# Sixty-four-row transposes for the inverse softmax sums, and a second output bank in the second layer's attention

## The reference

```python
def softmax_f32(s, dtype):
    return jax.nn.softmax(s.astype(jnp.float32), axis=-1).astype(dtype)

# layer of the first block, need_ctx = (it is not the last layer)
ya, yca = global_gqa(px[0], px[1], px[2], pc[0], pc[1], pc[2], cos, sin, qn, kn, need_ctx)
yb, ycb = neighbourhood_attn(px[3], px[4], px[5], pc[3], pc[4], pc[5], rpb, need_ctx)
yc_, ycc = window_gqa(px[6], px[7], px[8], pc[6], pc[7], pc[8], cos, sin, sink, need_ctx)
ux = jnp.concatenate([ya, yb, yc_], axis=-1) * jax.nn.silu(px[9])
x = x + gate[:, None, :] * (ux @ w_out)
```

## Time and profile before

| | us |
|---|---|
| median of 3 runs | 1854.64 |
| lowest, highest | 1851.79, 1855.0 |
| the profiled execution | 1852.03 |
| its span in the trace | 1850.2 |
| PE busy, share of the span | 1817.2, 98% |
| DVE busy, share | 1261.6, 68% |
| ACT busy, share | 1083.4, 59% |
| mean granted clock of PE | 0.997 of full speed |

### The profile page before, as it was taken

How to read it: one execution, slowest core, us unless ns; L and a number is a source line. 1 busy time by engine, 2 the same in 40 slices (tenths; PEclk the granted TensorE clock), 3 DMA queues, 4 the chain that set the end, 5 groups by cost and what they waited for, 6 DMA issues and landing times.

```text
span 1850.2 us, 34397 instructions
## 1 busy us (share of the span) xinstructions
PE 1817.2 (98%) x13400; PEld 1577.4 (85%) x13400; DVE 1261.6 (68%) x2157; ACT 1083.4 (59%) x1907; POOL 55.0 (3%) x57
## 2 busy tenths in 40 slices
PE   7999999999999999999999999999999999999998
PEld 5878878879888978889889988889888889998887
DVE  6663354478726678776686787757776677688765
ACT  5372264385736487764656577746774556567762
POOL 0000000003000000001000000000000000000001
PEclk9999999999999999999999999999999999999999
DMA  9232243242234315555432445554554642355553
GB/s 356 101 115 84 98 157 112 92 145 98 86 113 143 118 67 182 192 194 208 182 115 92 173 179 194 181 199 173 191 187 173 220 156 93 137 182 182 182 184 134
DMA packets 42571, 285.49 MB, mean 154 GB/s; under 512 B 4944, under 2 KB 6352, under 8 KB 9424
## 3 DMA queue, kind: packets, MB, share of 16 engines
q1 hardware_dynamic: 40832, 278.24, 41.9%
q0 software_dynamic: 1616, 5.52, 0.9%
HBM read 282.69 MB, written 1.05 MB: 153 GB/s over the span
## 4 chain that ended last, share of the span: by engine, by line
PE 92%; ACT 3%; DVE 2%; issue 1%; DMA 1%; SPq 0%; POOL 0%; DVEq 0%; ACTq 0%
PE bank L2340 25%; PE bank L2334 14%; PE bank L2335 13%; PE bank L2336 13%; PE bank L2341 13%; PE bank L2607 3%; PE bank L2553 3%; PE bank L2521 2%; PE bank L2438 1%; ACT work L1101 1%; PE bank L2508 1%; DMA token_major<-weights 1%; DVE panels_lo L1508 1%; ACT token_major L1079 1%; PE bank L2535 1%
## 5 line engine op out<-in xcount | busy, mean ns | idle before, releaser
L2340 PE MATMUL bank<-acts,panels_hi 128*128 128x512 f32 x2032 | 710.6, 396 | 0.5 <-DVE panels_lo L1508 0.5
L1508 DVE TENSOR_TENSOR panels_lo<-raw_panels,panels_hi 128x1024 fp32r<-128x1024 f32 x468 | 573.0, 1242 | 188.2 <-ACT panels_hi L954 186.5
L954 ACT ACTIVATE panels_hi<-raw_panels 128x1024 fp32r<-128x1024 f32 x468 | 484.4, 1054 | 248.3 <-PE bank L2336 152.5
L2341 PE MATMUL bank<-acts,panels_lo 128*128 128x256 f32 x2032 | 565.3, 278 | 0.0
L2340 PEld LDWEIGHTS bank<-acts,panels_hi 128*128 128x128 f32 x2032 | 381.3, 188 | 91.6 <-DVE panels_lo L1508 1.3
L2341 PEld LDWEIGHTS bank<-acts,panels_lo 128*128 128x128 f32 x2032 | 382.2, 188 | 0.1
L2334 PE MATMUL bank<-acts,panels_hi 128*128 128x256 f32 (+1 forms) x1120 | 350.9, 313 | 1.1 <-DVE xT L1587 0.4
L2335 PE MATMUL bank<-acts,panels_hi 128*128 128x256 f32 (+1 forms) x1120 | 345.8, 309 | 0.0
L2336 PE MATMUL bank<-acts,panels_lo 128*128 128x256 f32 (+1 forms) x1120 | 345.7, 309 | 0.0
L2334 PEld LDWEIGHTS bank<-acts,panels_hi 128*128 128x128 f32 x1120 | 213.4, 191 | 18.1 <-issue 4.5
L2336 PEld LDWEIGHTS bank<-acts,panels_lo 128*128 128x128 f32 x1120 | 213.5, 191 | 10.8
(11 more groups left out here) (304 smaller groups left out, 1868.7 us busy)
## 6 DMA issues: line engine op xcount, KB each, us to landing
raw_panels<-weights SPq DMA_DIRECT2D x252, 1024.0 KB, 4.8
token_major<-weights SPq DMA_DIRECT2D x4, 1024.0 KB, 9.0
near_bias<-rpb POOLq DMA_DIRECT2D x12, 256.0 KB, 3.7
xT<-xin SPq DMA_DIRECT2D x4, 512.0 KB, 5.6
gates<-weights SPq DMA_DIRECT2D x2, 1024.0 KB, 10.1
near_bias<-weights SPq DMA_DIRECT2D x4, 512.0 KB, 7.3
token_major<-weights SPq DMA_DIRECT2D x2, 512.0 KB, 12.6
token_major<-rpb POOLq DMA_DIRECT2D x4, 256.0 KB, 2.8
```

The source lines that it names most:

```text
L954: act.activation(slot_hi(n, a, b), raw_of(n, a, b), ACT.Copy).then_inc(hi_ready, 1)
L1508: dve.tensor_tensor(slot_lo(n, a, b), raw_of(n, a, b), slot_hi(n, a, b).bitcast(F32), ALU.subtract).then_inc(lo_ready, 1)
L2340: pe.matmul(bank.rearrange("p (c t) -> p c t", c=2), whi_, with_rest(xhi_), start=start, stop=False, skip_group_check=True)
L2341: return pe.matmul(bank[:, 0:T], wlo_, xhi_, start=False, stop=stop, skip_group_check=True)
```

## The change

Three parts.

1. **Halves of the spread.** For every deferred step but the last of a stage, the 128x128 transposes of the inverses become transposes of 64 rows each, in the tile shape of the turns. The upper halves stand in the turns of the following step, behind the first two turns of its second head; the lower halves behind its last turn (and behind the signal to ACT). A new semaphore, `half_spread` (inverses_turned_by_half), keeps the two halves of a bank apart: the lower ones wait until the upper ones are complete. The waits for `normed`, `omul` and the gate's last quarter move with the upper halves. `to_columns` is cut into products of 64 columns and moves behind the values' products.
2. **A second output bank.** In the second layer of the first block pairs use banks 6 and 7 in turn, so a new pair waits for the pair before the last.
3. **The last quarter of gates** goes to bank 7 in all of the second layer; in mixers B and C it is multiplied in two parts, 5 of 8 blocks in iteration 1 and 3 in iteration 2 behind the turns, and its tanh and product move from iteration 2 to 3.

```diff
+def late_in_two(m, l):
+
+    return l == 1 and not late_part(m, l)
...
-    out_bank = banks[6]
+    def second_bank(blk, st):
+
+        return blk == 1 and st.layer == 1
+
+    def out_bank(blk, st, pair):
+        return banks[7 if second_bank(blk, st) and pair % 2 else 6]
 
     def late_bank(m, l):
-        return banks[7 if late_part(m, l) else 6]
+        return banks[7 if l else 6]
...
-        def to_columns(rows, dst):
+        def to_columns(rows, dst, width=P):
 
             for e in range(2):
-                o = pe.matmul(dst[:, 2 * e:2 * e + 2], rows[:, e * P:(e + 1) * P], const("sel"),
-                              start=True, stop=True, skip_group_check=True)
+                for c in range(0, P, width):
+                    o = pe.matmul(dst[c:c + width, 2 * e:2 * e + 2], rows[:, e * P + c:e * P + c + width], const("sel"),
+                                  start=True, stop=True, skip_group_check=True)
...
             def out_bank_free(j):
 
-                if late and j == 0:
+                pair = steps[j].pair
+                if late and steps[j].first and pair == (1 if second_bank(blk, st) else 0):
                     pe.wait_ge(gate_last_out, late)
-                if steps[j].first and p0 + steps[j].pair >= 1:
-                    pe.wait_ge(omul, now(omul, p0 + steps[j].pair))
+                if steps[j].first and p0 + pair >= 1:
+                    pe.wait_ge(omul, now(omul, p0 + pair - (1 if second_bank(blk, st) and pair else 0)))
                 if steps[j].deferred:
                     pe.wait_ge(normed, now(normed, 2 * (g0 + j) + 2))
 
-            def whole_spread(j, k):
-
-                q0 = T + steps[j].deferred[k][1]
-                pe.transpose(out_bank[:, q0:q0 + P], inverse_rows(blk, g0 + j, k), ident)
+            def spread(j, h):
+
+                rows = slice(h * HD, (h + 1) * HD)
+                for k, q0 in steps[j].deferred:
+                    a = T + q0 + h * HD
+                    o = pe.transpose(out_bank(blk, st, steps[j].pair)[:, a:a + HD], inverse_rows(blk, g0 + j, k)[rows],
+                                     ident[rows, h * HD:(h + 1) * HD])
+                return o
...
                 if late and i == 1:
-                    last_gate(mixer, st.layer)
+                    last_gate(mixer, st.layer, range(6, NB) if late_part(mixer, st.layer) else range(0, 5 if st.layer else NB))
...
-                        for c, d in un.blocks:
+                        for n, (c, d) in enumerate(un.blocks):
                             turn_probs(g, e, c, d, 0)
                             o = turn_probs(g, e, c, d, 1)
+                            if e and n == 0 and j and steps[j - 1].deferred:
+                                out_bank_free(j - 1)
+                                if halves.n:
+                                    pe.wait_ge(half_spread, halves.n)
+                                spread(j - 1, 0).then_inc(half_spread, 1)
                     o.then_inc(probT, 1)
+                    if j and steps[j - 1].deferred:
+                        pe.wait_ge(half_spread, halves.n + 1)
+                        spread(j - 1, 1).then_inc(half_spread, 1)
+                        halves.n += 2
+                if late and i == 2 and late_in_two(mixer, st.layer):
+                    last_gate(mixer, st.layer, range(5, NB))
```

More of the change, by code:

```diff
@@ L385, in program @@
     near_hi = sem("near_queries_keys_hi")
+    half_spread = sem("inverses_turned_by_half")
     scores, negmax, exped, normed = sem("scores"), sem("negmax"), sem("exped"), sem("probs_normed")
@@ L1058, in attention, with last_tanh @@
             for i in range(len(steps) + 6):
-                if late and i == 2:
+                def last_tanh():
                     act.wait_ge(gate_last, late)
@@ L1062, in attention @@
                     act.activation(gates[:, 1536:1536 + w], late_bank(mixer, st.layer)[:, 0:w], ACT.Tanh, scale=0.5).then_inc(gate_tanh, 1)
+                if late and i == 2 and not late_in_two(mixer, st.layer):
+                    last_tanh()
                 for r, slot in enumerate(ADA_SLOTS[mixer] if st.panels and blk == 1 else ()):
@@ L1084, in attention @@
                     o.then_inc(probT_out, 1)
+                if late and i == 3 and late_in_two(mixer, st.layer):
+                    last_tanh()
                 if blk == 1 and 3 <= i + sooner < 5:
@@ L1786, in attention @@
                     m.then_inc(negmax, 1)
-                if late and i == 2:
+                if late and i == (3 if late_in_two(mixer, st.layer) else 2):
                     dve.wait_ge(gate_tanh, late)
@@ L2364, in feature_major, with last_gate @@
             return o
-        def last_gate(m, l):
+        def last_gate(m, l, blocks):
             w = 2 * T if l == 0 else T
-            part = late_part(m, l)
-            feature_major(ONE["gate" + m, l].at["panels"] + 1, late_bank(m, l)[:, 0:w], 1,
-                          lambda b: (act_x(ahi, 1, b, 0, w), act_x(alo, 1, b, 0, w)),
-                          range(6 if part else 0, NB), begins=not part).then_inc(gate_last, 1)
+            o = feature_major(ONE["gate" + m, l].at["panels"] + 1, late_bank(m, l)[:, 0:w], 1,
+                              lambda b: (act_x(ahi, 1, b, 0, w), act_x(alo, 1, b, 0, w)),
+                              blocks, begins=blocks[0] == 0, ends=blocks[-1] == NB - 1)
+            if blocks[-1] == NB - 1:
+                o.then_inc(gate_last, 1)
         def feature_major_rest(n, bank, m, rhs, inputs=None, blocks=range(NB)):
@@ L2509, in turn @@
             o.then_inc(turned, 1)
+        halves = Chain(half_spread)
         def attention(blk, mixer, with_ctx, st, ahead):
@@ L2583, in attention @@
                         branch_gate(st, r)
-                for r, slot in enumerate(ADA_SLOTS[mixer] if st.panels and blk == 1 else ()):
-                    row = ADA_ROW[mixer] + r
-                    if i == slot + 2:
-                        pe.wait_ge(row_out, row + 1)
-                        c = MOD_COLS + 4 * row
-                        to_columns(cmpw[:, 0:PW], banks[7][:, c:c + 4]).then_inc(row_turned, 1)
                 j = i - 3
@@ L2596, in attention @@
                         pe.wait_ge(last_weighed, 1)
-                    else:
+                    elif j == len(steps) - 1 or not step.deferred:
                         out_bank_free(j)
-                        for k in range(len(step.deferred)):
-                            whole_spread(j, k)
+                        if step.deferred:
+                            whole_spread(j)
                     pe.wait_ge(probT_out, now(probT_out, g + 1))
@@ L2610, in attention @@
                 if far_tail and j == len(steps) - 2:
-                    g = g0 + len(steps) - 1
-                    pe.wait_ge(normed, 2 * g + 2)
-                    pe.transpose(out_bank[:, T + P:2 * T], inverse_rows(blk, g, 0), ident).then_inc(last_inverse, 1)
+                    pe.wait_ge(normed, 2 * (g0 + len(steps)))
+                    whole_spread(len(steps) - 1).then_inc(last_inverse, 1)
+                for r, slot in enumerate(ADA_SLOTS[mixer] if st.panels and blk == 1 else ()):
+                    row = ADA_ROW[mixer] + r
+                    if i == slot + 2:
+                        pe.wait_ge(row_out, row + 1)
+                        c = MOD_COLS + 4 * row
+                        to_columns(cmpw[:, 0:PW], banks[7][:, c:c + 4], HD).then_inc(row_turned, 1)
                 if blk == 1 and i >= len(steps):
```

22 lines of the change are left out of this document (13 added, 9 removed).

## The result

The changed kernel takes **1858.68 us** (median of 20 runs, 1857.03 to 1860.53) where the kernel before takes 1853.88 (20 runs, 1849.67 to 1855.17). The ratio is 1.0027, with a 95% interval of 1.0021 to 1.0033: slower by 4.8 us. The forecast of no change was wrong. The profiled execution took 1860.53 us, its span is 1858.7; that of before was 1850.2.

A forecast was written before the change was run, and what follows sets the result against it. PE was taken to bound the kernel, busy for 98% of the span. The terms -3.4 - 0.7 + 0.5 + 3.6 summed to 0.0 us, so the forecast was 1854.6 us, no change, range 1850.2 to 1858.7.

The forecast's parts named there:

- halves, savings and earlier waits, first block: First block's attention steps: 26 steps save 0.13 us each, 3.4 gained; earlier waits for the freed bank lose 0.5.
- columns: Column products behind the values, 8 records of 64: 0.46 us as before, so nothing gained or lost.
- second bank: Second layer's mixers: waits for the product that frees the bank go, but ACT's copy comes last next, so no gain.
- gate in parts, with the bank: Second layer's mixers B and C: waits of 0.36 and 0.37 us for ACT's first copy end, 0.7 us gained.
- second block, waits and what follows: Second block: PE waits in the turns, gate 2.0 us later, 0.3 given back, next step loses 0.1; 3.6 for both layers.
- second block, clock: Behind the second block's new wait: the sum counted no loss from a clock fall and left one to a rival.
- Rival 2: Second block, both layers: the clock falls behind the new wait, costing 2 x 1.7 = 3.4 us, 1858.0; chance 0.16.
- The step on the halves: Spread in halves: each half transpose costs 0.06 us, the lower half's wait 0, so a step saves 0.13.
- the term for the earlier waits in the first layer: First layer: waits for the freed bank move into the turns; eight places lose 0.5 us together, 0.15 at 117.05.

The follow-up runs named there:

- e6: The changed kernel with no halves at all; columns, second output bank and gate in parts stay: 1851.52 us, ratio to before 0.9989.
- e5: The kernel before with halves of the spread in the first block and nothing else: 1856.88 us, ratio 1.0018.
- e4: The kernel before with the columns as 8 records of 64 behind the values and nothing else: 1849.95 us, ratio 0.9980.
- e11: The kernel before with the second output bank in the second layer, last gates of mixers B and C there in one part: 1852.58 us, one run.
- e3: The changed kernel with the branch gate's first 12 products done ahead of the second block's long wait and again behind it: 1856.37 us, ratio to before 1.0017.
- e2: The kernel before with halves of the spread in the second block and nothing else: 1859.72 us, ratio 1.0038.
- e7: The changed kernel with the first 24 of the branch gate's 48 products ahead of the second block's long wait, none repeated: 1851.56 us, ratio to before 0.9989.
- e8: The kernel before with the columns as 8 records of 64 at their old place ahead of the spread: 1851.60 us, ratio 0.9990.

## Why the prediction was wrong

| step | forecast | measured | from |
|---|---|---|---|
| halves, savings and earlier waits, first block | -3.4 + 0.5 | +0.3 beside the rest, +3.4 alone | changed and e6; e5 |
| columns | 0 | -2.9 | e4 |
| second bank | 0 | 0.0 | e11 |
| gate in parts, with the bank | -0.7 | -0.6 | e6 |
| second block, waits and what follows | +3.6 | +4.6 | e3, e2's second layer |
| second block, clock | 0, a rival with a chance of 0.16 | +3.0 | changed, e3 |
| sum | 0.0 | +4.4 by the trace, +4.8 by the medians | |

**The step that failed is the one on the clock in the second block, which the sum put at 0.** The place, the releaser and the mechanism of the wait were right: 2.0 us later was forecast for the gate and 2.2 measured, and with the steps around it a layer lost 2.3 and not 1.8, so 4.6 in place of 3.6 for both. But the fall of the clock behind it was left to a rival. The argument against it was that no wait of 0.8 us in the second layer had brought one. That argued from waits half as long, while the earlier trace rows had shown a fall behind waits. Three of the four waits of 1.6 us in the second block were followed by a fall. Rival 2 put it at 1.7 us each and 1858.0; measured were 1.5 and 1858.68, and that its time came so near is in part luck, since other terms of its sum were off by 3 us and cancelled. The Trainium skill's rule beside it (TensorE: Matmul & The Clock Gate, section PE-mode transpose), that transposes don't count as activity for the clock, isn't told apart by these runs: the products of e3 took away both the stillness and the neighbourhood of transposes. The stops of 1.45 to 1.62 us ahead of turns in the first block, with no fall behind them, don't speak for it.

**The step on the halves failed in its two assumptions of size.** The price of a half, 0.06, was right (0.065). "The lower half waits until the upper one is complete ... I put it at 0" was wrong: 0.08, more than half of the 0.13 saved. And the term for the earlier waits in the first layer priced eight places at 0.5 together; seven waits with 3.2 us stand in e5's first layer where two with 0.5 stood. At 117 us alone, where 0.15 was forecast, e5 loses 0.30 and the changed kernel 0.67. It should have followed the wait step by step, since the product that frees the bank comes as late at each new pair. In the changed kernel part of this loss is the columns' too, since they no longer cover the wait (e4 gives back 0.27 at the first long wait of mixer A).

**The term for the columns failed in size.** The nearest row was the values' 0.064 a record. Eight records of it gave 0.51; 0.33 (width alone) and 0.28 (behind the values) were measured, the second even under the lower bound of 0.30. I had not counted the change of shape: in the values' own tile shape behind the values, a group starts 0.1 us sooner.

The two large errors in the first block had opposite signs: 3.2 too much gain from the halves, 2.9 too little from the columns. That they cancelled is luck, and so the second block alone decided. The second bank and the gate's parts came out as forecast, though the gate's gain was put down to the parts alone and needs the bank.

Five kernels beat both, before and changed. The best two are the columns alone (0.9980) and the changed kernel with the spread left whole in the second block (0.9981); e6 and e7 (0.9989 each) and e8 (0.9990) are closer to before.

## What to carry to other kernels

When an instruction with a wait moves ahead of a long group of products, price three things: the wait that the group had covered, the waits of all later steps of the same kind, and the clock. A short stop of PE can be paid twice; if the stop can't go, a piece of the work behind it put ahead of it took away 3.0 of 3.8 us a layer here. Of small groups of PE, the columns gained 1.7 us by their width alone and 2.9 with a place next to a group of their own tile shape, where making the transposes smaller gave nothing.

## What the runs showed of the hardware

**Dense products in two paces.** Between 690 and 850 us all kernels run the same pairs of products (512 and 256 columns) at a granted clock of 1.00, without a wait. Timeline of PE in the kernel before:

```profile
780.20 0.40 PE L2340 MATMUL bank<-acts,panels_hi 128*128 128x512 f32 x1
...
783.67 0.40 PE L2340 MATMUL bank<-acts,panels_hi 128*128 128x512 f32 x1
```

In the kernel with the columns alone:

```profile
779.65 0.40 PE L2357 MATMUL bank<-acts,panels_hi 128*128 128x512 f32 x1
...
781.77 0.40 PE L2357 MATMUL bank<-acts,panels_hi 128*128 128x512 f32 x1
```

Ten pairs from 780.20 to 783.67 are 0.347 us each, six from 779.65 to 781.77 are 0.353. The pace stays the same for the whole stretch, and the slower one costs 2.95 us there; the table's column 662 to 951 shows it in nine of the eleven kernels listed, and before, e2 and e6 have the faster one (e6's profiled execution took 1847.25 us, the lowest of its 11, with a median of 1851.52). The run times of one kernel have single values about 3 us under the others (1846.5 and 1847.4 for the columns alone, with a median of 1849.95), which would fit a pace that differs from execution to execution too; what sets it was not tried and stays open.

**Clock falls in unchanged code** stood near 125, at 427 to 433, at 931 to 935 and near 1510 us in single traces, 1.0 to 1.8 us each, in stretches whose code was the same in traces without them. The one near 1510 stands in three of the four traces with halves in the second block and in none of the ten others; whether the change brings it there stays open. So a single profiled execution of this kernel is good to 3 or 4 us as a whole and to 0.1 in its parts, and the parts are what to compare.

**A half transpose** of 64 rows costs 0.065 us after its like, a whole one 0.11. A change of the tile shape cost PE about 0.1 us in two neighbourhoods: behind the values (the next group after 1.03 us, and after 0.93 in the same shape) and behind the turns (16 turns take 0.60 us to the whole transpose, where ten take 0.31 to a half one).
